# Opening, recurrence, conformer output and last group of a two-layer decoder trunk, reordered; hi and lo products of whole groups kept apart

## The reference

```python
for i in range(2):
    hn = rms_norm(h, norm_mix_g[i])
    mix = conv_recurrent_mixer(hn, ...) if i == 0 else stick_breaking_mixer(hn, ...)
    h = h + mix
    h = h + squared_relu_mlp(rms_norm(h, norm_mlp_g[i]), w_mlp_up[i], w_mlp_down[i])   # 2048 -> 8192 -> 2048
    gate = sigmoid(rms_norm(h, norm_ple_g[i]) @ w_ple_gate[i])
    h = h + (p[i] @ w_ple_proj[i]) * gate
return rms_norm(h, norm_f_g)
```

## Time and profile before

| | us |
|---|---|
| median of 3 runs (lowest, highest) | 2388.08 (2386.59, 2389.94) |
| profiled execution | 2388.35 |
| its span | 2386.6 |
| TensorE busy | 2336.7 (98%) |
| VectorE busy | 1575.7 (66%) |
| ScalarE busy | 1276.1 (53%) |
| data moved | 439.46 MB, mean 184 GB/s |

### The profile page before, as it was taken

How to read it: one execution, slowest core, us unless ns; L and a number is a source line. 1 busy time by engine, 2 the same in 40 slices (tenths; PEclk the granted TensorE clock), 3 DMA queues, 4 the chain that set the end, 5 groups by cost and what they waited for, 6 DMA issues and landing times.

```text
span 2386.6 us, 39036 instructions
## 1 busy us (share of the span) xinstructions
PE 2336.7 (98%) x13578; PEld 2048.7 (86%) x13578; DVE 1575.7 (66%) x1894; ACT 1276.1 (53%) x1606; POOL 22.7 (1%) x31
## 2 busy tenths in 40 slices
PE   7999999999999999999999999999999999999997
PEld 6888988888888888888888888888888888888886
DVE  6889986656655555667776666766556556556665
ACT  5676575444444445555565666555445445445553
POOL 0001100000000000000000000000000000000000
PEclk9999999999999999999999999999999999999998
DMA  6659856556556555555655545656565565555543
GB/s 216 204 149 216 221 167 192 190 187 189 189 187 191 186 189 188 185 191 169 194 176 172 169 153 174 195 184 195 186 192 186 188 190 186 191 186 184 193 160 105
DMA packets 440595, 439.46 MB, mean 184 GB/s; under 512 B 13392, under 2 KB 438480, under 8 KB 440528
## 3 DMA queue, kind: packets, MB, share of 16 engines
q1 hardware_dynamic: 432080, 430.20, 56.8%
q0 software_dynamic: 8448, 8.39, 2.6%
HBM read 428.05 MB, written 2.10 MB: 180 GB/s over the span
## 4 chain that ended last, share of the span: by engine, by line
PE 85%; DVE 6%; DMA 4%; ACT 2%; issue 2%; DVEq 0%; SPq 0%; ACTq 0%
PE ps L439 53%; PE ps L445 26%; PE ps L437 2%; DVE spl L1107 2%; DMA spl<-raw 2%; DMA raw<-in_w_out 1%; PE ps L443 1%; ACT spl L705 1%; DVE y L1447 0%; DMA raw<-in_w_in 0%; DVE tv L1143 0%; PE O L568 0%; PE Z L542 0%; DMA raw<-in_w_o 0%; PE Z L551 0%
## 5 line engine op out<-in xcount | busy, mean ns | idle before, releaser
L1107 DVE TENSOR_TENSOR spl<-raw,spl 128x1024 fp32r<-128x1024 f32 x794 | 959.7, 1223 | 535.1 <-ACT spl L705 504.7
L705 ACT ACTIVATE spl<-raw 128x1024 fp32r<-128x1024 f32 x826 | 857.6, 1054 | 673.4 <-PE ps L445 589.0
L439 PE MATMUL ps<-XA,spl 128*128 128x512 f32 x3072 | 973.3, 398 | 26.0 <-DVE spl L1107 17.6
L439 PE MATMUL ps<-XB,spl 128*128 128x512 f32 x2944 | 926.0, 396 | 2.7 <-ACT pp L705 2.7
L445 PEld LDWEIGHTS ps<-XA,spl 128*128 128x128 f32 x3072 | 580.4, 189 | 137.6
L445 PEld LDWEIGHTS ps<-XB,spl 128*128 128x128 f32 x2944 | 553.0, 188 | 130.7
L445 PE MATMUL ps<-XA,spl 128*128 128x256 f32 x3072 | 606.3, 279 | 0.0
L445 PE MATMUL ps<-XB,spl 128*128 128x256 f32 x2944 | 578.4, 278 | 0.0
L439 PEld LDWEIGHTS ps<-XA,spl 128*128 128x128 f32 x3072 | 471.5, 190 | 28.5 <-issue 11.5
L439 PEld LDWEIGHTS ps<-XB,spl 128*128 128x128 f32 x2944 | 448.2, 189 | 3.3 <-issue 2.9
L1143 DVE TENSOR_TENSOR tv<-cross,ps 128x512 f32<-128x512 f32 x199 | 135.7, 682 | 39.8 <-ACT cross L705 39.5
(11 more groups left out here) (161 smaller groups left out, 1084.9 us busy)
## 6 DMA issues: line engine op xcount, KB each, us to landing
raw<-in_w_up SPq DMA_DIRECT2D x256, 512.0 KB, 3.7
raw<-in_w_down SPq DMA_DIRECT2D x256, 512.0 KB, 3.8
raw<-in_w_qkv SPq DMA_DIRECT2D x96, 512.0 KB, 4.4
raw<-in_w_in SPq DMA_DIRECT2D x64, 512.0 KB, 4.7
raw<-in_w_gate SPq DMA_DIRECT2D x64, 512.0 KB, 4.3
raw<-in_w_out SPq DMA_DIRECT2D x32, 512.0 KB, 4.8
raw<-in_w_o SPq DMA_DIRECT2D x32, 512.0 KB, 4.5
spl<-raw POOLq DMA_DIRECT2D x16, 512.0 KB, 6.4
```

The lines of the kernel that those rows point to most:

```text
L439: pe.matmul(ps[:, b + o, :], w[:, q, 0, c], x[:, kt, :, :], start=start, stop=False)
L705: return act.activation(out, in_, ACT.Copy, scale=scale)
L1107: dve.tensor_tensor(s[:, :, 1, :], raw[:, m % NRAW, :, :], s[:, :, 0, :].bitcast(F32), ALU.subtract).then_inc(lo_ready, 1)
```

## The change

- Opening: x comes in five DMAs (two tiles, two, four, four, four), with the first chunks between them; the parameters come in two DMAs on ACT's queue; ACT runs one tiny Identity first. The squares of x go four tiles at a time to `pp`, which is free then, and are folded there by adds of four, two and one tile.
- The gate weights become chunks 16 and 17, behind the recurrence's groups 2 and 3; the `rg_head` matmuls move behind later groups. The first pairs of the recurrence are written out in a new order on all engines.
- The chain of exp, tanh, square and root product runs in halves of four tiles; the first half stands within the last pair of the recurrence. Splits, the square root and the scans are ordered anew in the first GLU pair.
- Conformer output: the copies of the embedding's products (`ple_out`) stand in another order on ACT; its first group waits for six of them instead of seven; its loop is written out.
- `whole`: in the MLPs, the attention's output projection and the gates a group issues all its matmuls of 512 columns and then all of 256. Exceptions are `first_pair` and the first group of each down projection.
- The last group of all runs `by_halves`: first 128 of its output channels, then the other 128, each with its own chain (`last_gate`). The output is scaled and stored in pieces of 5, 5, 4 and 2 tiles.

The diff, cut (eight columns of indentation are left out; `decay_rates` holds the lines that stood before the pairs, `rg_exp` and `rg_tanh` take their half of the tiles, `gemm` got the arguments `releases` and `sums`; `cuts`, `group` and the rest are unchanged):

```diff
 G_REC, C_REC = 0, 2
-C_RG = 8
...
...
-        sp.dma_start(h[:, 4 * k:4 * k + 4, :], xT[4 * k * P:(4 * k + 4) * P, :].rearrange(
+        t0, t1 = ((0, 2), (2, 4), (4, 8), (8, 12), (12, 16))[k]
+        sp.dma_start(h[:, t0:t1, :], xT[t0 * P:t1 * P, :].rearrange(
             "(t p) n -> p t n", p=P)).then_inc(x_landed[k], 16)
...
     load_x(0)
-    sp.dma_start(params[:, :], par).then_inc(par_landed, 16)
-    load_first(0)
+    load_first(0, (0,))
     load_x(1)
+    load_first(0, (1,))
+    load_x(2)
     load_first(1)
-    load_x(2)
     load_x(3)
+    load_x(4)
     load_first(2)
     load_first(3)
+    for s in range(2):
+        load_group(8 + 4 * s, 0, w_in[0], 256 + 2 * DA + s * DB)
     for j, w in enumerate((w_rg_a, w_rg_x)):
         m = C_RG + j
         sp.wait_ge(lo_ready, m - NRAW + 1)
         dst = raw[:, m % NRAW, :, :].rearrange("p a (b n) -> p (a b) n", b=2)
         sp.dma_start(dst, w[0].rearrange("h i j -> i h j")).then_inc(raw_landed[m % NRAW], 16)
...
+    with sp.Fori(2, 4) as i:
         load_group(C_REC, i, w_in[0], i * 256 + 2 * DA)
...
+    for q, (t0, t1) in enumerate(OUT_PIECES):
         sp.wait_ge(out_ready, q + 1)
-        sp.dma_start(outT[4 * q * P:(4 * q + 4) * P, :].rearrange("(t p) n -> p t n", p=P),
-                     h[:, 4 * q:4 * q + 4, :]).then_inc(stored, 16)
+        sp.dma_start(outT[t0 * P:t1 * P, :].rearrange("(t p) n -> p t n", p=P),
+                     h[:, t0:t1, :]).then_inc(stored, 16)
     sp.wait_ge(stored, 64)
...
+    def whole(g, gi, m, it, x, tiles=None):
+        b = 2 * (g % 2)
+        if counts(g - 1, gi):
+            pe.wait_ge(sum_ready, gi + (g - 1))
+        for j in range(4):
+            if tiles is not None:
+                pe.wait_ge(*tiles[j])
+            pe.wait_ge(hi_ready, it * 8 + (m + j + 1))
+            for q in range(4):
+                for o in range(2):
+                    hi_product(b, m + j, q, o, x, 4 * j + q, j == 0 and q == 0, False)
+        for j in range(4):
+            lo_there(pe, m + j, it)
+            for q in range(4):
+                for o in range(2):
+                    mm = lo_product(b, m + j, q, o, x, 4 * j + q, j == 3 and q == 3, False)
+            mm.then_inc(chunk_used, 1)
...
         first_pair(g, m, x, after_res(f_in), lambda: stats(norm))
         with pe.Fori(1, 4) as i:
             for s in range(2):
-                gemm(g + s, i * 2, m + 4 * s, i, x)
...
+                whole(g + s, i * 2, m + 4 * s, i, x)
+        tiles = [(up_tiles, u + 2 * j + 2) for j in range(4)]
+        gemm(g + 8, 0, m + 32, 0, hid, tiles)
+        whole(g + 9, 0, m + 36, 0, hid)
+        with pe.Fori(1, 4) as i:
+            for s in range(2):
+                whole(g + 8 + s, i * 2, m + 32 + 4 * s, i, hid)
...
+    def by_halves(g, m, x):
+        b = 2 * (g % 2)
+        pe.wait_ge(sum_ready, g - 1)
+        for o in range(2):
+            c = slice(o * P, (o + 1) * P)
+            for j in range(4):
+                lo_there(pe, m + j, 0)
+                w = spl[:, (m + j) % NSPL, :, :, c]
+                for q in range(4):
+                    pe.matmul(ps[:, b + o, :], w[:, q, 0, :], x[:, 4 * j + q, :, :],
+                              start=(j == 0 and q == 0), stop=False)
+                for q in range(4):
+                    mm = pe.matmul(ps[:, b + o, 0:256], w[:, q, 1, :], x[:, 4 * j + q, 0, :],
+                                   start=False, stop=(j == 3 and q == 3))
+            mm.then_inc(half_done, 1)
...
+        with pe.Fori(1, 3 if halves else 4) as i:
+            for s in range(2):
+                whole(g + s, i * 2, m + 4 * s, i, x)
+        if halves:
+            whole(g + 6, 0, m + 24, 0, x)
+            by_halves(g + 7, m + 28, x)
...
                                stop=(a == 1 and n == 2), skip_group_check=True)
         mm.then_inc(rg_done, 1)
+    gemm(G_REC + 2, 0, 8, 0, XA, mid=lambda: stats(0))
+    gemm(G_REC + 3, 0, 12, 0, XA, releases=3)
+    gemm(G_REC + 4, 0, C_REC + 16, 0, XA)
     pe.wait_ge(lo_ready, C_RG + 2)
-    gemm(G_REC + 2, 0, C_REC + 8, 0, XA, mid=lambda: stats(0))
-    gemm(G_REC + 3, 0, C_REC + 12, 0, XA)
     rg_head(0, 0)
     rg_head(0, 1)
-    for i in range(2, 4):
-        for s in range(2):
-            gemm(G_REC + 2 * i + s, 0, C_REC + 8 * i + 4 * s, 0, XA)
-            rg_head(i - 1, s)
+    gemm(G_REC + 5, 0, C_REC + 20, 0, XA)
+    rg_head(1, 0)
+    rg_head(1, 1)
+    gemm(G_REC + 6, 0, C_REC + 24, 0, XA)
+    rg_head(2, 0)
+    gemm(G_REC + 7, 0, C_REC + 28, 0, XA)
...
     ple(G_PLE0, C_PLE0, 0, range(8))
-    with pe.Fori(0, 2) as i:
-        for s in range(4):
-            gemm(G_OUTA + s, i * 4, C_OUTA + 2 * s, i, XB, [(ya_tiles, 1), (ya_tiles, 2)], (0, 4))
+    for s in range(NG):
...
+        act.wait_ge(sum_ready, g)
+        for o in range(2):
+            act.wait_ge(half_done, o + 1)
+            copy(cross[:, o, :], ps[:, 2 * (g % 2) + o, 256:512]).then_inc(half_cross, 1)
+            act.wait_ge(half_scaled, o + 1)
+            act.activation(tv[:, o, :], tv[:, o, :], ACT.Sigmoid).then_inc(half_sig, 1)
+            if o == 1:
+                act.activation(rC[:, 0:1], epsb[:, :], ACT.Sqrt)
+            act.wait_ge(half_h, o + 1)
+            act.activation(tv[:, o, :], h[:, 14 + o, :], ACT.Square).then_inc(half_sq, 1)
+            act.wait_ge(half_sq, o + 1)
+            act.activation(h[:, 14 + o, :], h[:, 14 + o, :], ACT.Identity,
+                           scale=gain(n, 14 + o)).then_inc(out_scaled, 1)
...
+    act.dma_start(params[:, 0:CONV_A_W], par[:, 0:CONV_A_W]).then_inc(par_landed, 16)
+    act.dma_start(params[:, CONV_A_W:], par[:, CONV_A_W:]).then_inc(par_rest, 16)
     act.wait_ge(consts_ready, 2)
+    act.activation(small[:, 3, 0:1], epsb[:, :], ACT.Identity)
     act.wait_ge(par_landed, 16)
-    def square_x(f):
-        if f >= 1:
-            act.wait_ge(sq_folded, 2 * f)
-        squares(2 * f)
+    def square_x(k):
+        act.activation(pp[:, 4 * k:4 * k + 4, :], h[:, 4 * k:4 * k + 4, :], ACT.Square).then_inc(sq_ready, 2)
...
     for k in range(4):
-        act.wait_ge(x_landed[k], 16)
         for f in (2 * k, 2 * k + 1):
+            act.wait_ge(x_landed[f if k == 0 else k + 1], 16)
             res_his(2 * f, 0, XA)
         split(2 * k)
-        if k >= 2:
+        split(2 * k + 1)
+        if k >= 1:
             square_x(k - 1)
-        split(2 * k + 1)
-        if k == 1:
-            square_x(0)
+    square_x(3)
+    act.wait_ge(par_rest, 16)
...
-        if c >= 2:
-            head_sigmoids(c - 2)
+        head_sigmoids(c - 2)
         round_x(c)
         for q in range(6, 8):
             split(m + q)
+        if c == 3:
+            rg_exp(0)
+            rg_tanh(0)
         take_cross(G_REC + 2 * c + 1, 0, group_done(C_REC + 8 * c + 4, 0))
...
-    rg_exp()
+    for m in range(8, 12):
+        split(m)
+    take_cross(G_REC, 0, (chunk_used, 7))
+    for m in range(12, 14):
+        split(m)
+    take_cross(G_REC + 1, 0, (chunk_used, 8))
+    for m in range(14, 16):
+        split(m)
+    norm(0)
+    split_rg(0)
+    split_rg(1)
+    split(18)
+    take_cross(G_REC + 2, 0, (chunk_used, 12))
+    split(19)
+    round_x(0)
+    gelu_gate(0)
+    for m in range(20, 24):
+        split(m)
+    round_x(1)
+    split(24)
+    take_cross(G_REC + 3, 0, (chunk_used, 16))
+    split(25)
+    gelu_gate(1)
+    rec_pair(2)
+    rec_pair(3)
+    head_sigmoids(2)
+    head_sigmoids(3)
     split(C_GLU + NSPL)
-    rg_tanh()
+    rg_exp(1)
     split(C_GLU + NSPL + 1)
+    rg_tanh(1)
     split(C_GLU + NSPL + 2)
+    take_cross(G_GLU, 0, group_done(C_GLU, 0))
     split(C_GLU + NSPL + 3)
-    take_cross(G_GLU, 0, group_done(C_GLU, 0))
-    act.wait_ge(rg_vec, 3)
+    split(C_GLU + NSPL + 4)
+    act.wait_ge(rg_vec, 6)
     act.activation(mlt[:, :, :], mlt[:, :, :], ACT.Sqrt).then_inc(rg_act, 1)
-    period(C_GLU + 4, 0)
+    split(C_GLU + NSPL + 5)
     take_cross(G_GLU + 1, 0, group_done(C_GLU + 4, 0))
+    split(C_GLU + NSPL + 6)
     glu_gate(0)
+    split(C_GLU + NSPL + 7)
...
+        ple_out(G_PLE0, C_PLE0, 0, ((2, 3), (6,))[k])
         act.wait_ge(ln_act, 3 + 2 * k)
         copy(XB[:, 4 * k:4 * k + 4, 0, :], y[:, 4 * k:4 * k + 4, :]).then_inc(ln_act, 1)
-        ple_out(G_PLE0, C_PLE0, 0, (3 + 2 * k,))
-    ple_out(G_PLE0, C_PLE0, 0, (6, 7))
+        ple_out(G_PLE0, C_PLE0, 0, ((4, 5), (7,))[k])
     period(C_PLE0, 0, 5)
...
+        for o in range(2):
+            v, t = tv[:, o, :], 14 + o
+            dve.wait_ge(half_cross, o + 1)
+            dve.tensor_tensor(v, cross[:, o, :], ps[:, 2 * (g % 2) + o, 0:256], ALU.add).then_inc(half_step, 1)
+            dve.wait_ge(half_step, 2 * o + 1)
+            dve.tensor_tensor(v, v, rB[:, :], ALU.mult).then_inc(half_scaled, 1)
+            dve.wait_ge(half_sig, o + 1)
+            dve.tensor_tensor(v, v, pp[:, t, :], ALU.mult).then_inc(half_step, 1)
+            dve.wait_ge(half_step, 2 * o + 2)
```

(117 more changed lines are left out.)

158 lines of the change are left out of this document (77 added, 81 removed).

## The result

The changed kernel takes 2374.72 us (2371.25 to 2375.27) against 2388.78 us (2386.59 to 2389.94) of the kernel before: 14.1 us less by the medians; the ratio of the runs is 0.9933 with a 95% interval of 0.9921 to 0.9944, which is 13 to 19 us less. The forecast was 2377.2 (range 2362 to 2394, faster 0.70). The profiled execution went from a span of 2386.6 to 2373.5, 13.1 less.

What follows compares the result with a forecast made beforehand. TensorE, busy 98% of the span, was taken as the bound. Savings 2.0 + 0.85 + 2.6 + 1.7 + 1.9 + 0.25 + 0 + 0 + 1.6 = 10.9 took 2388.35 to 2377.4, median 2377.2 us; range 2362 to 2394.

Steps and rivals of the forecast that it cites:

- The bound: Whole kernel: TensorE is busy 98%; time can come only from its idles, its lower clock or a matmul's length.
- Opening, -2.0: Recurrence's projection: with new squares and adds, VectorE frees the bank sooner; chunk 8 starts at 38.3 for 40.34, -2.0 us.
- Clock behind it, -0.85: After chunk 8's idle: whether the clock falls again could not be told; half of 1.7 us was counted, -0.85.
- Second and third stall, -2.6, -1.7, -1.9: Recurrence's projection: idle of 2.59, the half-clock stretch behind it and idle of 1.91 go: -2.6, -1.7, -1.9 us.
- Recurrence in halves, -0.25: Recurrence chain up to 244 us: GLU waits shrink but mostly return later; -0.25 us, bounds -3 and +2.
- Conformer output, 0: Stage before MLP 0: TensorE may start earlier but restarts at 358.06 as before; 0, bounds -1.5 and +1.
- from there the stage runs at DVE's pace: Conformer output from 309.6: one VectorE sum per 5.63 us against 5.58 of matmuls sets the pace.
- opening rival: Opening: a new wait eats the gain, second to third stall halved, first unchanged; 4.8 left, 2384 or so, 17%.
- Whole groups, 0: 134 groups, 2144 quads reordered: the quad's sum of 0.697 us is conserved, so order is worth 0; ends +28 and -64.
- the alternation costs: Rival for whole groups: a 512 in a run takes 0.2267, a quad 0.6933; -8 us, 2369, 15%.
- The end, -1.6: Last group by halves: 4.4 us instead of 6.03 before the last statistics; -1.6 us, bounds -2.4 and 0.
- the page's price: Recurrence in halves: priced by the skill page, the extra table change costs 2.7 us, making this term about +1.1.

Runs made afterwards that it cites:

- experiment 5: The kernel after with the opening's squares as before (pairs of tiles into tv, two adds each on VectorE), gate weights still later: 2370.87 us.
- Experiment 6: The kernel after, but ScalarE rounds the first recurrence tiles and takes the first GELU ahead of gate weights and chunks 18 and 19, as before: 2371.57 us.
- experiment 11: The kernel after with the recurrence's exp and tanh in one piece again and the conformer output's order as before: 2371.31 us.
- the repeat: The kernel after run again unchanged (also called 9), as base on the chip of the three runs that follow it: 2372.86 us.
- experiment 12: The kernel after with first sum taken early, chunks 79 and 81 subtracted on VectorE, unread matmuls before the last tiles' convolution and MLP 0: 2367.24 us.
- experiment 7: The kernel after with chunks 79 and 81 subtracted on VectorE instead of their lo part being added up by DMA: 2372.67 us.
- experiment 3: The kernel after with the whole groups reordered by chunk, eight hi products then eight lo products: 2380.53 us.
- experiment 4: The kernel after with the last group of the last gates taken as all others, not by halves, output pieces unchanged: 2375.22 us.
- 1: The kernel after with hi and lo products of every group but the last mixed again as before: 2375.26 us.

## Why the prediction was right, and where it was not

**The bound.** Held: only TensorE's idles, its clock and the length of a matmul moved the time.

**Opening, -2.0.** Measured -3.0, and the step that named its cause failed ("four squares of 1024 elements into pp, three adds"): experiment 5 gives the squares +0.8, and -3.8 to the three subtractions fewer with the earlier start. I had summed VectorE's new list from 28.2 on (10.0; it took 9.7 from 27.57) and set it against 40.34 without asking what the old list would do with the same subtractions out. The old adds of 0.42 fitted into idle VectorE time; three adds of 1.22 did not.

**Clock behind it, -0.85.** Measured 0: the stretch came again here, after 3.12 of idle. In the other traces it came at this place after 2.15 and after 2.82 to 5.33, and did not after 2.11 and 2.19. My list of restarts also lacked one of the kernel before, 2.42 idle before 246.87, which no fall followed. "Whether it falls I cannot tell" was the right statement; half its price was fair.

**Second and third stall, -2.6, -1.7, -1.9.** Right: the idles and the stretch at 61.5 are gone, 6.4 from chunk 8 to the first GLU group for 6.2. Experiment 6 shows that they stay away with the old order on ScalarE as well; that the two extra chunks ahead did it is what is left, not shown by itself. That the whole opening came to 9.4 for 9.05 is luck in part: 1.0 too little for the first stall and 0.85 too much for its clock.

**Recurrence in halves, -0.25.** From the first GLU group to the last tiles' convolution the kernel gained 0.4, near the forecast, but not for its reason: the halves cost 1.1 by experiment 11, so the new order of splits, root and scans, which that experiment keeps in the main, gained some 1.5. No run tests that order alone. The restart at 135.41 waits for the sum of the first GLU group, whose cross part ScalarE takes at 132.22 in the repeat
```profile
111.38 1.28 ACT L994 ACT_TABLE_LOAD   x1
112.67 1.71 ACT L994 ACTIVATE dec<-rg,nlamc 128x256 f32<-128x256 f32 x4
...
119.86 0.63 ACT L962 ACTIVATE pp<-tv 128x512 f32<-128x512 f32 x1 [2.09 <-DVE tv L1245]
...
132.22 0.58 ACT L773 ACTIVATE cross<-ps 128x512 f32<-128x512 f32 x1
```
and at 130.01 in the kernel of experiment 11, whose GELU comes 5.4 earlier:
```profile
114.46 0.63 ACT L962 ACTIVATE pp<-tv 128x512 f32<-128x512 f32 x1 [1.53 <-DVE tv L1245]
...
130.01 0.57 ACT L773 ACTIVATE cross<-ps 128x512 f32<-128x512 f32 x1
```
Against the one half that is done early stand one more table load and VectorE's and ScalarE's waits for each other around it; net 2.2 later on ScalarE, 1.1 on VectorE's take (134.81 for 133.73). I had walked that chain with the old clock and had seen the first GLU wait shrink by 0.7.

**Conformer output, 0.** The step "from there the stage runs at DVE's pace" was right for this kernel: starting the stage earlier bought nothing at MLP 0. With the earlier waits relieved it does (experiment 12: 344.41 there for 350.11). But 2.75 were given back between the last tiles' convolution and MLP 0, and two causes are known. The weights did not come 9.8 earlier: ScalarE began to round chunk 83 at 270.87 for 278.83, 8.0 earlier, and had waited 6.81 for it (5.23 before) with the 16 DMA engines at 0.96; taking two accumulating DMAs away removed that wait and 1.1 of the loss (experiment 7). And the new order itself cost about 1 (experiment 11). The repeat gave back 1.7, so 1.0 of the 2.75 came and went between two executions of one kernel. My opening rival named neither; it expected the loss at chunk 18.

**Whole groups, 0.** The mis-sized term: -4.4, the small form of the rival "the alternation costs" (forecast -8). The step "If the sum is what is conserved, a 512 is really (0.697 - 0.240)/2 = 0.2285 and order is worth nothing" failed: a 512 is 0.2333 in pairs and 0.227 in a long run, a 256 0.115 and 0.120, so a 512 gains 6 ns where a 256 loses 5. Over a run of 32 a 512 takes 0.2275, 1 ns under 0.2285, and my own measure, 4.3 us for each ns of a 512, gives the 4.4 back. But that rival was not right as a mechanism either, for by chunk there are fewer changes of width than in pairs, and it is slower (experiment 3).

**The end, -1.6.** Right: -1.6, experiment 4 has 1.9. The idle before the last statistics is 4.18 for 4.4 foreseen. Its chain, against the earlier trace rows:
```profile
2358.15 1.28 ACT L925 ACT_TABLE_LOAD   x1
...
2359.44 0.20 ACT L925 ACTIVATE rC<-epsb 128x1 f32<-128x1 f32 x1
2359.55 0.40 ACT L927 ACTIVATE tv<-h 128x256 f32<-128x256 f32 x1
2359.98 0.43 DVE L1383 TENSOR_TENSOR nacc<-nacc,tv 128x256 f32<-128x256 f32 x1 [0.94 <-ACT tv L927]
```
VectorE waits 0.94 there for the square that sits behind the load; the forecast had 0.6 for it. The next activation stands 0.01 behind the load's end. By the Trainium skill, "ScalarE: Activation LUTs", "What ACT_TABLE_LOAD costs", a drain about as long as the load comes with it; the trace again shows no room for one, since the activation ahead of it (2357.72, 0.42 long) ends as it starts. That the page's price made the halves +1.1, which is what they measured, is therefore chance.

## What to carry to other kernels

Price a moved step against the old list without the other edits too, one at a time: here one edit's gain hid another's loss, and kernels with one edit less (experiments 5 and 11) were no slower. What is gained upstream is only worth what the next rate-bound stretch (here the DMAs at 0.96 and VectorE's one sum per 5.6 us) lets through; look for that stretch first, and relieve it together with the gain. When executions differ by amounts like the effect, compare landmarks of traces whose clock is alike, not medians.

## What the runs showed of the hardware

- Matmuls from start to start depend on their neighbours: 512 columns (the hi and the lo part of an activation) take 233.3 ns in pairs with 256s and 227 from the sixth in a run on, 256 columns 115 in pairs and 120 in a run, each matmul with weights of its own. The Trainium skill, "TensorE: Matmul & The Clock Gate", "Back-to-back issue gap", has N/2.4 + 2.5 ns, that is 216 and 109, which it calls the gap of an isolated matmul, without a budget for the weight load; no order here reaches either. Why the first five of a run differ was not tried.
- An idle of TensorE of 1.8 us or more (up to 5.3) can be followed by a stretch of 3.4 us at 1.2 GHz (once 6.8), and the same idle is not always: at MLP 0, after 2.55 to 2.57, it came in three traces out of eight (in the kernel after and experiments 5 and 7, not in 1, 3, 4, 6 and 9), and the kernel after and its repeat differ in it with the same code. No stretch came in the trace with the idles filled.
- A byte that a DMA adds to a tile from another tile on the chip took 2.5 times the engine time of one that is only loaded from memory (2.3 to 2.4 in the same window of the repeat and of experiment 7). The DMA view of the kernel after from 230 to 270 us (queue, packets, MB, share of 16 engines; q0 is the queue that GpSimd issues to, with the accumulating DMAs):
```profile
q0 software_dynamic: 3157, 3.14, 58.3%
q1 hardware_dynamic: 4720, 4.93, 37.1%
```
